# One encoder layer on one core: the last stage summed from rows stacked on 96 partitions in column strips, and a routing with fewer linked operations

## What is computed

```
g_logits = xt @ w_rg + b_rg ;  e_logits = xt @ w_re + b_re       # 4 and 32 columns
group = argmax(g_logits) ; the two best experts inside it, with weights w0, w1 = softmax(top two) * softmax(g)[group]
f(token) = w0 * E_a(token) + w1 * E_b(token),  E(x) = (silu(x @ w_gate) * (x @ w_up)) @ w_down
out = LN(alpha * x1 + (1 + gate(c)) * f(u)) * ln2_g + ln2_b
```

## Time and profile before

| | |
|---|---|
| median of 3 runs | 1517.87 us (1516.25 to 1518.43) |
| profiled execution, its own time | 1519.21 us |
| its span, first to last instruction | 1517.3 us |
| mean granted TensorE clock | 0.991 |
| PE / PEld / DVE / ACT / POOL busy | 97% / 53% / 37% / 23% / 6% |
| DMA, mean over the span | 201 GB/s |
| routing (DVE L2128 to the first turned row block on PE) | 839.4 to 873.2 us |
| expert turns | 875.6 to 1461.3 us |
| last stage | 1464.4 us to the end |

### The profile page before, as it was taken

The page is one execution under the profiler, slowest core; times in us unless marked ns, Lnnn a source line. Parts: engine busy times, 40 slices in busy tenths (PEclk is TensorE's granted clock), DMA queues, the critical chain, the costliest instruction groups (busy, mean ns, idle before and its releaser), DMA issues. The chain is left out here.

```text
span 1517.3 us, 19808 instructions
## 1 busy us (share of the span) xinstructions
PE 1466.9 (97%) x7315; PEld 808.6 (53%) x7316; DVE 564.5 (37%) x1133; ACT 351.8 (23%) x739; POOL 98.6 (6%) x98
## 2 busy tenths in 40 slices
PE   7999999999989999999999899999999999999997
PEld 4555554447768666665555544444444444444443
DVE  2222117556879443436777700111111111011128
ACT  1112122137734343433111011111111110111111
POOL 0000002000000000000000111111111111111110
PEclk9999999999999999999999899999999999999999
DMA  9401001128840300004111599879789879999965
GB/s 342 165 28 42 0 1 36 45 55 237 265 128 1 118 0 0 0 0 166 60 56 70 222 383 394 321 287 413 314 329 418 320 311 412 425 369 413 424 282 202
DMA packets 101797, 305.49 MB, mean 201 GB/s; under 512 B 18353, under 2 KB 61661, under 8 KB 92536
## 3 DMA queue, kind: packets, MB, share of 16 engines
q1 hardware_dynamic: 93064, 287.08, 49.3%
q0 software_dynamic: 8064, 16.80, 3.0%
q10 hardware_dynamic: 624, 1.03, 0.2%
HBM read 289.86 MB, written 25.76 MB: 208 GB/s over the span
## 5 line engine op out<-in xcount | busy, mean ns | idle before, releaser
L2009 PE MATMUL ps<-w_down_sb,hidT 128*128 x320 | 153.4, 612 | 0.0
L462 PE MATMUL ps<-w_in_tok,uT 128*128 128x512 f32 (+2 forms) x384 | 141.5, 529 | 0.0
L1993 PE MATMUL ps<-w_gate_sb,x_slotsT 128*128 x320 | 140.7, 593 | 0.7 <-ACT x_slotsT L2092 0.7
L1993 PE MATMUL ps<-w_up_sb,x_slotsT 128*128 x320 | 140.6, 592 | 0.0
L1664 PE MATMUL ps<-uT,hT 128*128 128x512 f32 x256 | 112.9, 594 | 0.3 <-ACT hT L1604 0.3
L632 PE MATMUL ps<-uT,mod 128*128 128x512 f32 x256 | 111.0, 593 | 0.8 <-PEq L218 0.8
L2248 DVE TENSOR_TENSOR hid<-silu_g,ps 128x512 f32<-128x512 f32 x20 | 13.7, 687 | 258.5 <-PE ps L1993 258.5
L462 PEld LDWEIGHTS ps<-w_in_tok,uT 128*128 128x128 f32 x384 | 72.6, 190 | 65.5 <-issue 43.9
L1993 PEld LDWEIGHTS ps<-w_gate_sb,x_slotsT 128*128 128x128 f32 x320 | 60.7, 190 | 76.9 <-issue 76.9
L1993 PEld LDWEIGHTS ps<-w_up_sb,x_slotsT 128*128 128x128 f32 x320 | 60.8, 190 | 76.5 <-issue 76.5
L2009 PEld LDWEIGHTS ps<-w_down_sb,hidT 128*128 128x128 f32 x320 | 55.8, 189 | 65.1 <-issue 64.3
(11 more groups left out here) (431 smaller groups left out, 1892.9 us busy)
## 6 DMA issues: line engine op xcount, KB each, us to landing
light_gate_sb<-in_w_gate SPq DMA_DIRECT2D x20, 2048.0 KB
light_up_sb<-in_w_up SPq DMA_DIRECT2D x20, 2048.0 KB
light_down_sb<-in_w_down SPq DMA_DIRECT2D x20, 2048.0 KB
w_gate_sb<-in_w_gate SPq DMA_DIRECT2D x12, 2048.0 KB
w_up_sb<-in_w_up SPq DMA_DIRECT2D x12, 2048.0 KB, 17.9
w_down_sb<-in_w_down SPq DMA_DIRECT2D x12, 2048.0 KB, 23.2
mod<-in_w_ada SPq DMA_DIRECT2D x8, 1024.0 KB, 9.0
w_ada_late<-in_w_ada SPq DMA_DIRECT2D x8, 1024.0 KB, 7.2
```

The costliest lines, as they stand in the source:

```text
L462: mm = nc.tensor.matmul(ps[:, 2 + g, 0:n], self.uT[:, k, t * P:(t + 1) * P], wt[:, k, c0:c0 + n], start=k == 0, stop=k == KD - 1)
L1993: m = m_.matmul(ps[:, bank, :], xT[:, k, :], wt[:, bass.ds(buf, 1), k, :].rearrange("p a f -> p (a f)"), start=k == 0, stop=k == KD - 1)
L2009: m = m_.matmul(ps[:, 5 + half, :], hT[:, k, :], wd[:, bass.ds(buf, 1), k, half * 512:half * 512 + 512].rearrange("p a f -> p (a f)"), sta ...
```

## The change

Router bias: an extra matmul with one row (a row of ones against the bias row) opens each tile's logits, and the DVE addition is gone. Routing: scans and casts are merged, the first heavy expert is found on one partition between other work, the routing weights are worked out last, and the slot map is used before the table's columns are finished; PE's `keep_clocked(7, 3)` moves ahead of the table's product, and PE and ACT read the number of turns after their first row block. Last stage: of each tile, 32 partitions hold expert 0's rows, 32 expert 1's, 32 x1's, each partition four rows of 4 KB; four matmuls of 96 rows and 32 columns (one per strip of 32 tokens) make each half of the sum; ACT does sum, mean, squares and root for tiles 0 to 6, DVE those of tile 7; `keep_clocked(4, 8)` comes ahead of the first sum.

```diff
@@ PE, logits(t) @@
+                        pe.wait_ge(s_br, 32)
+                    m_.matmul(ps[:, 6, 0:NG + E], self.cst[0:1, C_ONE:C_ONE + P], self.br[0:1, :], start=True, stop=False)
...
-                        m = m_.matmul(ps[:, 6, 0:NG + E], uT[:, k, :], wr[:, k, :], start=k == 0, stop=k == KD - 1)
+                        m = m_.matmul(ps[:, 6, 0:NG + E], uT[:, k, :], wr[:, k, :], start=False, stop=k == KD - 1)
@@ experts: names @@
-        yb = self.ybuf.rearrange("(t p k) d -> t p k d", p=P, k=2)
+        yb = self.ybuf.rearrange("(t s p k) d -> t k p s d", s=4, p=LC, k=2)
+        x1b = self.x1d.rearrange("(t s p) d -> t p s d", s=4, p=LC)
...
+            strips = lambda buf: buf.rearrange("p (s d) -> p s d", s=4)
+            homes = [strips(buf[:, j].rearrange("p k f -> p (k f)")) for buf in (wg, wu) for j in range(2)]
+            homes += [strips(buf[:].rearrange("p k f -> p (k f)")) for buf in (lwg, lwu, lwd)]
+            rows3 = lambda t: homes[t % len(homes)]
@@ SP, last loads @@
-                for t in range(TT):
-                    sp.dma_start(x1[:, t], self.x1d[t * P:(t + 1) * P, :]).then_inc(s_x1[t], 16)
-                sp.wait_ge(s_yfree, n + 1)
-                sp.wait_ge(s_lyfree, n + 1)
-                for t in range(TT):
-                    sp.dma_start(yt(t), yb[t]).then_inc(s_y[t], 16)
+                for t, (s_free, freed) in enumerate(((s_G, n + 1), (s_G, n + 1), (s_U, n + 1), (s_U, n + 1), (s_lG, n + 1), (s_lG, n + 1), (s_lY, n + 1), (s_sum, 1))):
+                    if t == TT - 1:
+                        sp.wait_ge(s_yfree, n + 1)
+                        sp.wait_ge(s_lyfree, n + 1)
+                        for u in range(t):
+                            for k in range(2):
+                                sp.dma_start(rows3(u)[k * LC:(k + 1) * LC], yb[u, k]).then_inc(s_y[u], 16)
+                    sp.wait_ge(s_free, freed)
+                    sp.dma_start(rows3(t)[2 * LC:3 * LC], x1b[t]).then_inc(s_x1[t], 16)
+                for k in range(2):
+                    sp.dma_start(rows3(TT - 1)[k * LC:(k + 1) * LC], yb[TT - 1, k]).then_inc(s_y[TT - 1], 16)
@@ PE, last stage @@
+                pe.wait_ge(s_dg, 1)
...
+                self.keep_clocked(4, 8)
                 for t in range(TT):
-                    rows_of_experts(t)
-                    if t + 3 < TT:
-                        residual(t + 3)
+                    rows_of_tile(t)
@@ PE, rows_of_tile(t) @@
+                    pe.wait_ge(s_x1[t], 16)
+                    pe.wait_ge(s_y[t], 32)
                     for half in range(2):
+                        for s in range(4):
+                            m = m_.matmul(ps[s * LC:(s + 1) * LC, SUM_BANKS[t % 4] + half, :], dg[0:3 * LC, 4 * t + s, :],
+                                          rows3(t)[0:3 * LC, s, half * 512:half * 512 + 512], start=True, stop=True)
@@ ACT, last stage @@
+                for t in range(TT - 1):
+                    act.wait_ge(s_sum, t + 1)
+                    a.activation(junk[0], bank_rows(t), ACT.Identity, accum_out=rsum[:, t:t + 1]).then_inc(s_mean, 1)
+                    act.wait_ge(s_mean, t + 1)
+                    a.mul(nmean[:, t:t + 1], rsum[:, t:t + 1], -1.0 / D).then_inc(s_nmean, 1)
+                    act.wait_ge(s_nmean, t + 1)
+                    a.activation(junk[1], bank_rows(t), ACT.Square, bias=nmean[:, t:t + 1], accum_out=sqs[:, t:t + 1]).then_inc(s_sq, 1)
+                    act.wait_ge(s_sq, t + 1)
+                    a.activation(std[:, t:t + 1], sqs[:, t:t + 1], ACT.Sqrt, bias=eps[:], scale=1.0 / D).then_inc(s_std, 1)
+                act.wait_ge(s_var, 1)
+                a.activation(std[:, TT - 1:TT], mv[:, 1:2], ACT.Sqrt, bias=eps[:]).then_inc(s_std, 1)
@@ DVE, routing @@
-                lk(v.tensor_tensor(self.lg[:], self.lg[:], self.br[:].unsqueeze(1).to_broadcast([P, TT, NG + E]), ALU.add))
...
-                lk(v.tensor_tensor_scan(bend[:], nbk[:], zero[:], 0.0, ALU.add, ALU.add))
-                lk(v.tensor_tensor_scan(lend[:], lt[:], zero[:], 0.0, ALU.add, ALU.add))
+                lk(v.tensor_tensor_scan(flat(ends[:]), flat(inside), flat(own), 0.0, ALU.mult, ALU.add))
...
-                lk(v.tensor_copy(lowf[:], low[:]))
-                lk(v.tensor_copy(colf[:], posi[:]))
@@ DVE, once before the turns @@
+                v.tensor_tensor(dg[0:3 * LC], i3[0:3 * LC].unsqueeze(1).to_broadcast([3 * LC, 4 * TT, LC]),
+                                w3[0:3 * LC].rearrange("p t s -> p (t s)").unsqueeze(2).to_broadcast([3 * LC, 4 * TT, LC]), ALU.mult).then_inc(s_dg, 1)
@@ DVE, last stage, per tile @@
+                    if t == TT - 1:
+                        dve.wait_ge(s_sum, t + 1)
                         cb.link(v.bn_stats(st[:, 0, :], sums(t, 0)))
                         cb.link(v.bn_stats(st[:, 1, :], sums(t, 1)))
                         cb.link(v.bn_aggr(mv[:], st[:].rearrange("p a b -> p (a b)")))
+                    else:
+                        dve.wait_ge(s_std, t + 1)
```

More of the change, by code:

```diff
@@ L1807, in experts @@
             ids = sb("ids", [P, 2, TT], I32)
-            idf, lowf, colf = (sb(n, [P, 2, TT]) for n in ("id_less_oob", "slot_row", "slot_column"))
+            idf = sb("id_less_oob", [P, 2, TT])
             at_row = [ys[:].rearrange("p (t q) -> p t q", t=TT), xT[:]]
@@ L1818, in experts @@
             eg = sb("e_gap", [P, TT])
-            cnt, nbk, bend, bst = sb("cnt", [P, E]), sb("nbk", [P, E]), sb("bend", [P, E]), sb("bst", [P, E])
+            cnt = sb("cnt", [P, E])
+            ends, begins = sb("block_ends", [P, 2, E]), sb("block_begins", [P, 2, E])
+            bend, bst, lend, lt = ends[:, 0], begins[:, 0], ends[:, 1], begins[:, 1]
+            first_c = sb("first_candidates", [1, E + 1])
             ci = sb("cnt_i", [P, E], I32)
             zero = sb("zero_e", [P, E])
-            hv, lt, lend = sb("is_heavy", [P, E]), sb("is_light", [P, E]), sb("light_end", [P, E])
+            hv = sb("is_heavy", [P, E])
             left, more, after = sb("experts_left", [P, E]), sb("has_next", [P, E]), sb("left_from", [P, E + 1])
@@ L2172, in _ @@
-                lk(v.tensor_scalar(lt[:], lt[:], float(LC), float(LB), ALU.mult, ALU.add))
-                lk(v.scalar_tensor_tensor(out=base[:], in0=bst[:], scalar=float(P), in1=lt[:], op0=ALU.mult, op1=ALU.subtract))
+                dve.wait_ge(s_firstc, 1)
+                v.tensor_reduce(first_c[:, E:E + 1], first_c[:, 0:E], AX, ALU.min).then_inc(s_firstc, 1)
+                lk(v.tensor_tensor(own[:, 0], ci[:], hv[:], ALU.mult))
+                lk(v.scalar_tensor_tensor(out=own[:, 1], in0=cnt[:], scalar=0.5, in1=hv[:], op0=ALU.is_gt, op1=ALU.subtract))
@@ new lines, in _ @@
+                dve.wait_ge(s_firstc, 2)
+                v.tensor_scalar_add(first_e[:], first_c[:, E:E + 1], 99.0).then_inc(s_first, 1)
+                flat = lambda buf: buf.rearrange("p a e -> p (a e)")
+                lk(v.tensor_tensor_scan(flat(ends[:]), flat(inside), flat(own), 0.0, ALU.mult, ALU.add))
+                lk(v.tensor_tensor(begins[:], ends[:], own, ALU.subtract))
+                lk(v.tensor_scalar(lt, lt, float(LC), float(LB), ALU.mult, ALU.add))
+                lk(v.scalar_tensor_tensor(out=base[:], in0=bst, scalar=float(P), in1=lt, op0=ALU.mult, op1=ALU.subtract))
@@ L2203, in _ @@
                 lk(v.tensor_scalar(left[:], after[:, 1:E + 1], -1.0, float(E), ALU.mult, ALU.add))
[L2204 to L2207 removed]
+                lk(v.tensor_scalar(cmp_[:, 0], bend, pcol, None, ALU.is_le))
+                lk(v.tensor_scalar(cmp_[:, 1], lend, pcol, None, ALU.is_le))
+                dve.wait_ge(s_map, 1)
+                lk(v.tensor_scalar_add(smap[:], ps[:, 3, 0:NCOL], float(OOB)))
+                v.tensor_scalar(tok[:], smap[:, 0:NB], 1, None, ALU.arith_shift_right).then_inc(s_asg, 1)
+                asgl4 = asgl[:].rearrange("p (c q) -> p c q", q=4)
+                for q in range(4):
+                    v.tensor_copy(asgl4[:, :, q], smap[q * LC:(q + 1) * LC, NB:]).then_inc(s_lasg, 1)
+                dve.wait_ge(s_lasg, 4)
+                v.tensor_scalar(tokl[:], asgl[:], 1, None, ALU.arith_shift_right).then_inc(s_lasg, 1)
+                lk(v.scalar_tensor_tensor(out=cmp_[:, 2], in0=bst, scalar=pcol, in1=hv[:], op0=ALU.is_le, op1=ALU.mult))
+                lk(v.scalar_tensor_tensor(out=cmp_[:, 3], in0=bst, scalar=pcol, in1=more[:], op0=ALU.is_equal, op1=ALU.mult))
                 lk(v.tensor_tensor(cmp_[:, 4], cmp_[:, 3], left[:], ALU.mult))
@@ L2210, in _ @@
                 v.tensor_scalar_min(col[:, 0:2], col[:, 0:2], float(E - 1)).then_inc(s_cols, 1)
+                for q in range(4):
+                    v.tensor_scalar(asgq[q * LC:(q + 1) * LC, :], asgl[:], 4.0, float(q), ALU.mult, ALU.add).then_inc(s_lasg, 1)
+                dve.wait_ge(s_rows, 1)
+                row = lambda j: ps[0:1, 2, j * NB:(j + 1) * NB]
+                for at, j in ((0, 0), (6, 1), (1, 2), (3, 3), (2, 4)):
```

(14 more changed lines are left out.)

120 lines of the change are left out of this document (37 added, 83 removed).

## The result

The changed kernel takes 1528.69 us (median of 4 runs, 1528.1 to 1530.23), the kernel before 1518.15 (median of 4, 1516.25 to 1519.5) beside it: ratio 1.0063, 95% interval 1.0048 to 1.0079, so 7 to 12 us slower. The forecast was 1519.2, and 1503.0 to 1524.5.

A forecast was written before the change was run, and what follows sets the result against it. PE, busy 97% of the span, was taken as the bound. Last stage +3.8 and routing with bias -2.5 made +1.3 us on the median 1517.87, so 1519.2; range 1503.0 to 1524.5.

The forecast's parts named there:

- half the rate into partitions 0 to 63: Last stage, expert-row loads: 64 partitions take half the rate, 5.0 us per tile; main case, chance 0.68.
- The last stage as a sum: Last stage: loads, PE's sums, DVE's last tile and store added up to an end at 1521.1, 3.8 us later.
- first tile at 1466.1 + 4.8 + 2.5: Last stage: old load issue time, landing delay and half-rate transfer put the first tile's rows at 1473.4.
- The clock: Last stage, PE's tile sum: 1.9 us, or 3.7 if its clock falls; 2.8 taken.
- The last store: End of last stage: 3.0 us from DVE's last work to span end, earlier tiles' stores done by 1520.
- The bias: Output projection: added matmul costs 1.5 to 3 us, dropped DVE addition saves 0.5; routing starts 1.0 later.
- The routing: Routing: shorter DVE chain and earlier gather start the first turn 2.5 us earlier, bias included, bounds 0 and 4.
- The expert turns (586 of the 1517 us) are therefore left alone by this change, apart from when they begin: Expert turns: PE waits only 2.9 us for light weights there, so their length was taken as unchanged.
- Full rate into 64 partitions: Rival, last-stage loads: the narrower width costs nothing, 2.5 us per tile, time 1504.5; chance 0.20.
- Strips do run side by side: Last-stage sums: strips side by side, 1.9 us per tile; rival without that 6.9, 1533.9, chance 0.07 with quarter rate.
- no change: Whole kernel: 1519.2 against a median of 1517.87, within the 3.0 us measurable; chance of same 0.44.

The follow-up runs named there:

- run 4: Changed kernel with expert 1's rows on partitions 64 to 95, issued by ACT instead of SP, and x1's on 32 to 63: 1523.39 us.
- run 5: Changed kernel without the x1 loads of the last stage and PE's waits for them (sums lack x1): 1526.93 us.
- run 6: As run 4, but x1 on partitions 96 to 127, products over 128 rows with weight 0 for 32 to 63: 1518.26 us.

## Why the prediction was wrong, step by step

**The rate: right.** The largest unknown, half the rate into partitions 0 to 63, came out as chosen: 208 GB/s, 5.07 us a tile where 5.0 was forecast. By the rule of the Trainium skill that the prediction cites ("SBUF — State Buffer", section "Door 1: The DMA port swizzle"), 64 low partitions reach half of the ports; the trace agrees, with 208, and so does run 4, with 320 into both halves. It doesn't account for the 135 to 138 of pieces for 32 to 63 by themselves.

**The last stage as a sum.** Its terms, from the end of the turns on:

| us | forecast | measured |
|---|---|---|
| end of turns to the first load's issue | 4.8 | 7.8 |
| to the first sum | 7.3 | 7.7 |
| six tiles | 30.0 | 30.4 |
| to the sum of tile 7 | 7.5 | 7.1 |
| that sum | 2.8 | 3.7 |
| DVE, last tile | 4.6 | 4.6 |
| to the end of the span | 3.0 | 4.0 |
| total | 60.0 | 65.3 |

(The prediction's own total is 59.8: its "1503.2" should be 1473.4 + 30.0 = 1503.4.)

The step that failed is "first tile at 1466.1 + 4.8 + 2.5": it kept 1466.1, the issue time of before, although the halved rate applies to the x1 loads too and they are still moving when the last scatter goes out. Before, they had landed by then. That is 2.9 of the 5.5 missing (65.3 less 59.8), and run 5 showed it: without them the loads come 4.94 after the turns, and the scatter lands in 3.21 instead of 6.21. The clock (0.9) was named and split down the middle; it stayed at 0.50, with PE busy 3.64 in each 5.07. The last store (1.0) I had called done; its queue was still full of earlier stores (421 GB/s from 1514 on).

**The bias: a size.** The mechanism was right, a product more in front of each tile with PE as the bound. I took 0.21 a tile from pure pace, and had 0.43 as the other end; it is 0.54, 0.34 for the product's own records, 0.10 more ahead of them and 0.10 more in the logits behind them (801.79 - 799.99 = 1.80, before 1.70). Six of them stand ahead of the last product of L1664 and make 3.2, all that P grew by. Behind it the last product, in the open, and the DVE addition that is saved cancel: from there to the first reduction it is 15.7 us in both kernels (839.92 - 824.2, 840.92 - 825.2). The forecast's + 1.0 was short by 2.2.

**The routing: a step.** DVE's chain came out: measured from the first reduction, POOL's issue (864.60 - 840.92 = 23.7 us, before 866.47 - 839.92 = 26.6) came 2.9 earlier, and the first turned rows 2.2 (31.0 against 33.2). The failed sentence is "The expert turns (586 of the 1517 us) are therefore left alone by this change, apart from when they begin". The gather landed 7.3 us after its issue (6.2 taken, 4.5 before), PE stood for it, and its clock, at which I had looked only for the slot map, fell where the turns begin. So 1.2 of the 2.2 were left, 2.3 less than the 3.5 forecast: 1.3 of it ahead of the turned rows, by the gather above all, 1.0 behind them.

**The rivals.** Full rate into 64 partitions is out (208 GB/s). Strips do run side by side: 16 records in 1.92 at full clock in run 6, 3.64 at half. The forecast's "no change" fell by three terms with one sign, +5.5, +2.2 and +2.3, none of which its range had summed: each bound had been taken for itself.
